# The decay matrix of the gated delta rule: eight broadcast products, or a scaled triangle and two wide ones

## The chip, the cores and the metric

The kernel runs on one core of one Trainium2 chip. The metric is the device time of one execution in microseconds. TensorE multiplies matrices, VectorE, ScalarE and GpSimd work element by element, and the sync engine's queue issues the weight transfers.

## The reference

A stack of blocks over 256 tokens with model width 1024: two mixer layers with a gated feed-forward block before and behind each, then an even and an odd mixer with their own feed-forward blocks. The weights, some 330 MB of f32, are read once. The change is in the mixer layer, in its gated delta rule branch. Cut to what matters:

```python
GDN_HEADS, GDN_DK, GDN_DV, GDN_CHUNK = 4, 128, 128, 64

def gated_delta_rule_chunked(q, k, v, beta, g):      # 256 tokens, 4 heads, chunks of 64
    gcum = jnp.cumsum(g, axis=-1)
    decay = jnp.exp(jnp.where(tril, gcum[..., :, None] - gcum[..., None, :], NEG_INF))
    a = jnp.where(strict, jnp.einsum('bhnid,bhnjd->bhnij', k_beta, k) * decay, 0.0)
    ...
    qk = jnp.einsum('bhnid,bhnjd->bhnij', q, k) * decay
```

The kernel works on blocks of 128 tokens rather than 64. There are eight blocks: 2 token tiles times 4 heads. For each it needs a 128x128 matrix whose entry (i, j) is the cumulated g up to token j, the same in every row i. With a 0/1 triangle T, that is the sum over tokens k of g[k] T[k, j].

## The kernel before

The whole kernel is one program of hand-ordered instruction streams, one for each engine, that wait for one another through semaphores. There is no planner.

*Weights.* They come as units of 128x1024 f32 (512 KB). The sync queue loads unit u into one of 3 raw buffers (L482) as soon as VectorE has split unit u-3. ScalarE copies it to `w_hi` (`split`, L539), rounding it, and VectorE subtracts to get the rest, `w_lo` (L1193). There are 6 slots of split weights, and the splits run 5 units ahead of TensorE (`AHEAD`). TensorE multiplies each unit in three passes, high by high, high by low and low by high (L2137 is the helper through which nearly all products are recorded). A unit of the gdn projection takes it 24 products of 256 columns.

*The mixer layer, as far as the change goes.* TensorE works through the units of `small`, `moba_q`, `gdn` (12 units), then a turn of latents (`cT`), four units `moba(1)`, the sums of squares `stat` (16 products with one column), the step `R`, the products of k with k (`G`), four units `moba(2)`, then the triangular solve. Meanwhile:

- VectorE computes g (`sc[:, 240:248]`, 128 tokens by 8 blocks; L1535 to L1543, event `g`), right before the pair loop over the gdn units. In each of the six rounds of that loop it splits two weight units (L1193), runs the convolution on two channels (L1559, six instructions of 256 columns) and the gating of the round before (L1570). After it come the last gating (event `silu`) and the rest of the latents (`c_lo`, L1596).
- ScalarE copies weights (L539) and the projection's results (L732, L735), and after `silu` squares q and k in one instruction (L769, event `gsq`). TensorE's `stat` waits for it.
- GpSimd computes reciprocal roots (L1108: `crs`, then `grs` after event `gvar`, which follows `stat`), and later in the solve five mask products of 128x512 (L1123). Between the mixers and the even mixer it prepares a filter with four products of 128x1024 (L1155).
- The step `R`: for each of the eight blocks TensorE loads the column of g, broadcast to 128 columns, as weights, and multiplies the 128x128 triangle `tri`. The result goes to banks 6 and 7 of PSUM. It waits for `c_lo`, which frees these banks. VectorE then forms the exponent in `E` (L1618, event `Et`).

Every f32 product (operands not rounded) shows as two records in the trace.

`arena[:, 3072:4096]` holds `zs` later in the layer (the z gate, written after the step QKT).

Of the kernel before, what the change touches and what calls it, by code (L numbers as in the profile page):

```python
# [21 lines left out]
ALU = mybir.AluOpType  # L22
AX = mybir.AxisListType

PART = 128
# [30 lines left out]
LEVELS = 7  # L56
# [162 lines left out]
class Events:  # L219
# [8 lines left out]
    def sig(self, l, step):  # L228
# [11 lines left out]
                "mlavark", "qrope", "mlak", "mlavarq"])  # L240
ACT_STEPS = (["sm", "spe", "csq", "cn", "egc", "kds", "c_hi", "gsq", "E", "AT", "QKT", ("U", 1), "mobasq"] + [s for s in LV_STEPS if s[0] == "U" and s[1] > 1]
             + ["u1", "wT", "O0", "osq", "mobaT", "oz_hi", "ksq", "qcopy", "qsq", "vcopy", "qT0", "qT1", "kT0", "kT1"])
POOL_STEPS = (["crs", "grs"] + [("ATM", m) for m in range(1, 4)] + ["mobars"] + [("ATM", m) for m in range(4, LEVELS - 1)]
              + ["ors", "mlarsk", "mlarsq"])


# [6 lines left out]
def build(nc, stream, params, consts, late_in, x_in, out):  # L253
    with ExitStack() as ctx:
        def sb(name, shape, dt=F32):
            return ctx.enter_context(nc.sbuf_tensor(name, shape, dt))

        def sem(name):
            return ctx.enter_context(nc.semaphore(name))
# [11 lines left out]
        ones = sb("ones", [PART, PART])  # L271
        nhalf = sb("nhalf", [PART, 64])
        sc = sb("sc", [PART, 512])
# [30 lines left out]
        act_ev = [Events(sem("act_step"), ACT_STEPS)]  # L304
        pool_ev = [Events(sem("pool_step"), POOL_STEPS)]
        PE, DV, AC, PO = pe_ev[0], dve_ev[0], act_ev[0], pool_ev[0]
# [41 lines left out]
        def const(name, i=0, n=None):  # L348
            lo, hi = CONST[name]
            return con[:, lo + i:(hi if n is None else lo + i + n)]  # L350
# [3 lines left out]
        def bank(b, lo=0, hi=512):  # L354
            return ps[:, b, lo:hi]

        def flat(ap):
            return ap.rearrange("p a b -> p (a b)")

        def over(ap, n):  # L360

            return ap.unsqueeze(2).broadcast_to([PART, ap.shape[1], n])

        def each(ap, n):

            return ap.unsqueeze(1).broadcast_to([PART, n, ap.shape[1]])


        def reg(lo, *dims):
            n = int(np.prod(dims))  # L370
            v = arena[:, lo:lo + n]
            return v if len(dims) == 1 else v.rearrange("p (a b) -> p a b", b=dims[-1])

        gup = gates[:, 8:24, :].rearrange("p a b -> p (a b)")
        mqkv = reg(0, 6, 512)
        zs = reg(3072, 4, TOK)
        y = reg(4096, 12, TOK)
        yth = reg(7168, 12, TOK)
        X, XTh = reg(7168, 8, 64), reg(7680, 8, 64)
# [18 lines left out]
        ATM = [tmpf[:, 0:1024].rearrange("p (a b) -> p a b", b=128), tmpf[:, 1024:2048].rearrange("p (a b) -> p a b", b=128)]  # L398
# [701 lines left out]
        @block.gpsimd  # L1100
        def _(pool):
            chain = [0]
            nc.gpsimd.memset(nhalf[:], -0.5).then_inc(pool_chain, 1)
            pool.wait_ge(pool_chain, 1)

            def rsqrt(o, i):
                n = i.shape[1]
                return nc.gpsimd.tensor_tensor(o, i, nhalf[:, 0:n], ALU.pow)  # L1108

            def norm(t):  # L1110
                pool.wait_ge(var_ready, t + 1)
                rsqrt(sc[:, 4:6], sc[:, 2:4]).then_inc(rs_ready, 1)

            def mixer(l):
                pool.wait_ge(*DV.at(l, "cvar"))
                rsqrt(sc[:, 228:232], sc[:, 224:228]).then_inc(*PO.sig(l, "crs"))
                pool.wait_ge(*DV.at(l, "gvar"))
                rsqrt(sc[:, 112:128], sc[:, 128:144]).then_inc(*PO.sig(l, "grs"))
                pool.wait_ge(*AC.at(l, "AT"))
                for m in range(1, LEVELS - 1):  # L1120
                    if m >= 3:
                        pool.wait_ge(*PE.at(l, ("U", m - 2)))
                    nc.gpsimd.tensor_tensor(ATMh[m % 2], ATh, each(const("mt", (m - 1) * 64, 64), 8), ALU.mult  # L1123
                                            ).then_inc(*PO.sig(l, ("ATM", m)))
                    if m == 3:
                        pool.wait_ge(*DV.at(l, "mobavar"))
                        rsqrt(sc[:, 192:224], sc[:, 160:192]).then_inc(*PO.sig(l, "mobars"))
                pool.wait_ge(*DV.at(l, "ovar"))
                rsqrt(sc[:, 152:160], sc[:, 144:152]).then_inc(*PO.sig(l, "ors"))
                pool.wait_ge(*DV.at(l, "mlavark"))  # L1130
                rsqrt(sc[:, 208:224], sc[:, 176:192]).then_inc(*PO.sig(l, "mlarsk"))
                pool.wait_ge(*DV.at(l, "mlavarq"))
                rsqrt(sc[:, 192:208], sc[:, 160:176]).then_inc(*PO.sig(l, "mlarsq"))

            t = 0
            for l in range(DEPTH):
                norm(t); t += 1
                norm(t); t += 1
                mixer(l)
                norm(t); t += 1  # L1140

            n_taps = 4 * TAP_STEP * TAP_GROUPS
            pool.wait_ge(mix_ready, 4 * DEPTH)
            nc.gpsimd.memset(wcomp, 0.0).then_inc(taps_set, 1)
            pool.wait_ge(taps_loaded, 16 * TAP_STEP)
            pool.wait_ge(taps_set, 1)
            for j in range(TAP_STEP):
                r, m = slice(TAP_ROWS * j, TAP_ROWS * (j + 1)), len(range(j, CFK, TAP_STEP))
                for i in range(4):
                    o = wcomp[r, TAP_STEP * TAP_GROUPS * i:TAP_STEP * TAP_GROUPS * (i + 1)].rearrange("p (q g) -> p q g", g=TAP_GROUPS)  # L1150
                    nc.gpsimd.tensor_copy(o[:, :, 0:m], wrep[r, :, CFK * i + j:CFK * (i + 1):TAP_STEP]).then_inc(taps_set, 1)
            pool.wait_ge(taps_set, 1 + 4 * TAP_STEP)
            for c in range(4):
                part = slice(n_taps // 4 * c, n_taps // 4 * (c + 1))
                nc.gpsimd.tensor_tensor(wtap[:, part, :], each(const("rows"), n_taps // 4), over(wcomp[:, part], TAP_ROWS), ALU.mult  # L1155
                                        ).then_inc(taps_set, 1)
            norm(t); t += 1

            pool.wait_ge(*DV2.at(0, "lnvar"))
            rsqrt(sc[:, 276:278], sc[:, 278:280]).then_inc(*PO2.sig(0, "lnrs"))  # L1160
            norm(t); t += 1
            norm(t); t += 1
            for i in "kq":
                pool.wait_ge(*DV2.at(0, f"dvar{i}"))
                rsqrt(drs[i], dss[i]).then_inc(*PO2.sig(0, f"drs{i}"))
            norm(t)
# [968 lines left out]
        def _(pe):  # L2135
            def mm(o, a, b, start=True, stop=True, **k):
                return nc.tensor.matmul(o, a, b, start=start, stop=stop, **k)  # L2137
# [241 lines left out]
            def mixer(l, t):  # L2379
                ev = lambda s, st: pe.wait_ge(*s.at(l, st))  # L2380
# [34 lines left out]
                for qk in range(2):  # L2415
                    for tt in range(2):
                        for h in range(4):
                            c = qk * 8 + tt * 4 + h
                            i = mm(bank(0, c, c + 1), tmp[:, qk * 4 + h, 128 * tt:128 * tt + 128], ones[:, 0:1])
                i.then_inc(*PE.sig(l, "stat"))  # L2420
                ev(DV, "c_lo")
                for b in range(8):
                    i = mm(bank(6 + b // 4, 128 * (b % 4), 128 * (b % 4) + 128), sc[:, 240 + b:241 + b].broadcast_to([PART, 128]), const("tri"))
                i.then_inc(*PE.sig(l, "R"))
                kT = lambda tt, h: y[:, 4 + h, 128 * tt:128 * tt + 128]
                qT = lambda tt, h: y[:, h, 128 * tt:128 * tt + 128]
# [49 lines left out]
                m = LEVELS - 1  # L2476
                ev(DV, ("X", m - 1))
                for b in range(8):
                    i = mm(ps[64:128, 1, 64 * b:64 * b + 64], ATx[0:64, b, :], X[0:64, b, :])
# [4 lines left out]
                for b in range(8):  # L2484
                    i = mm(ps[0:64, 4, 64 * b:64 * b + 64], U[64:128, b, :], XT[64:128, b, 64:128])
# [50 lines left out]
                for n in range(2):  # L2536
                    for j in range(TT):
# [4 lines left out]
                        i = mm(o, a_lo[:, 10, tk], w_hi[:, s, w], start=False, stop=True)  # L2542
# [6 lines left out]
                for j in range(TT):  # L2549
                    tk = slice(128 * j, 128 * j + 128)  # L2550
                    for k in range(2):
# [3 lines left out]
                        i = mm(o, a_lo[:, 8 + k, tk], w_hi[:, s, w], start=False, stop=(k == 1))  # L2555
# [218 lines left out]
            for l in range(DEPTH):  # L2774
                ffn(POS["ffa", l], F, t); F += FT; t += 1
                mixer(l, t); t += 1
                ffn(POS["ffb", l], F, t); F += FT; t += 1
# [121 lines left out]
```

## Time and profile before

| | |
|---|---|
| median of 3 runs | 1989.17 us (1986.13 to 1991.87) |
| span of the profiled execution | 1983.2 us |
| TensorE matmul busy | 1952.0 us (98%) |
| TensorE weight loads busy | 1818.2 us (92%) |
| VectorE busy | 1491.1 us (75%) |
| ScalarE busy | 1083.7 us (55%) |
| GpSimd busy | 96.1 us (5%) |
| mean granted TensorE clock | 0.996 |

The busy times are sums over the whole span. Engines work at the same time, and their waits are told apart by the chain of waits and the timeline. The granted clock is given as a share of full speed: 1.00 is 2.4 GHz, 0.50 is 1.2 GHz.

### The profile page before, as it was taken

To read this page: it belongs to the slowest core of one execution; us is meant where nothing else is said; L and a number is where in the kernel's file an instruction comes from. 1 tells how busy PE (TensorE), PEld (TensorE's weight loads), DVE (VectorE), ACT (ScalarE), POOL (GpSimd) and SP (SyncE) were. 2 spreads that over 40 slices of the span, in tenths; PEclk is the share of its full clock that TensorE was granted. 3 is DMA by queue.
4 is the path that set the end of the run, shared out by engine and by line. 5 is a ranking of instruction groups with operands and counts; after the bars stand their busy time and mean duration, and the time that the engine had idled before them with its cause. 6 is when DMAs were issued, how large, how long until landed. Compare 5 with 4: busy or idle time off the path is not lost.

```text
span 1983.2 us, 38420 instructions
## 1 busy us (share of the span) xinstructions
PE 1952.0 (98%) x14681; PEld 1818.2 (92%) x14681; DVE 1491.1 (75%) x2306; ACT 1083.7 (55%) x1714; POOL 96.1 (5%) x61
## 2 busy tenths in 40 slices
PE   9999999999999999999999999999999999999999
PEld 8999899999999999998899999999899999889998
DVE  6777877667777777778767778777578888877887
ACT  5455664664545554556546644555345555765554
POOL 0000002010000000000120103000000000100000
PEclk9999999999999999999999999999999999999999
DMA  6555443344555555555424454555745555534554
GB/s 228 184 185 194 161 155 108 108 156 146 158 188 189 193 167 184 188 170 181 140 85 141 142 170 151 192 187 178 211 163 179 190 183 167 170 127 139 191 190 138
DMA packets 95799, 331.04 MB, mean 167 GB/s; under 512 B 10960, under 2 KB 16720, under 8 KB 95568
## 3 DMA queue, kind: packets, MB, share of 16 engines
q1 hardware_dynamic: 93712, 325.91, 50.3%
q10 hardware_dynamic: 1984, 3.68, 0.5%
q8 instruction: 74, 1.21, 0.3%
q14 instruction: 29, 0.24, 0.0%
HBM read 327.91 MB, written 1.64 MB: 166 GB/s over the span
## 4 chain that ended last, share of the span: by engine, by line
PE 83%; DVE 8%; ACT 3%; DMA 2%; issue 1%; POOL 1%; SPq 0%; DVEq 0%; ACTq 0%
PE ps L2137 82%; DVE w_lo L1193 3%; DMA raw<-stream 2%; ACT w_hi L539 1%; POOL sc L1108 1%; ACT a_both L565 1%; DVE arena L1559 1%; PE ps L2348 1%; ACT tmp L568 0%; PE ps L2562 0%; DVE x L1204 0%; POOL tmp L1123 0%; DVE tmp L1289 0%; DMA x<-x_in 0%; PE ps L2715 0%
## 5 line engine op out<-in xcount | busy, mean ns | idle before, releaser
L2137 PE MATMUL ps<-a_both,w_hi 128*128 128x256 f32 (+1 forms) x7104 | 1402.9, 312 | 9.6 <-ACT a_both L565 3.0
L2137 PEld LDWEIGHTS ps<-a_both,w_hi 128*128 128x128 f32 x7104 | 1158.8, 191 | 85.4 <-ACT a_both L565 4.0
L2137 PE MATMUL ps<-a_both,w_lo 128*128 128x256 f32 x4464 | 978.5, 283 | 0.0
L1193 DVE TENSOR_TENSOR w_lo<-raw,w_hi 128x1024 fp32r<-128x1024 f32 x614 | 750.1, 1228 | 244.3 <-ACT w_hi L539 243.9
L2137 PEld LDWEIGHTS ps<-a_both,w_lo 128*128 128x128 f32 x4464 | 739.8, 191 | 8.9
L539 ACT ACTIVATE w_hi<-raw 128x1024 fp32r<-128x1024 f32 x614 | 634.4, 1050 | 160.9 <-DMA raw<-stream 102.5
L1108 POOL TENSOR_TENSOR sc<-sc,nhalf 128x2 f32<-128x2 f32 (+5 forms) x25 | 66.0, 2641 | 1656.8 <-DVE sc L1221 1223.4
L2137 PE MATMUL ps<-w_hi,a_both 128*128 128x512 f32 (+2 forms) x464 | 140.0, 379 | 4.1 <-DVE w_lo L1193 2.8
L608 ACT ACTIVATE a_both<-arena 128x256 fp32r<-128x256 f32 x132 | 55.2, 418 | 138.3 <-DVE arena L1310 108.1
L597 ACT ACTIVATE arena<-arena 128x256 f32<-128x256 f32 x88 | 36.8, 418 | 169.4 <-DVE arena L1302 143.9
L1267 DVE TENSOR_TENSOR arena<-ps,arena 128x512 f32<-128x512 f32 x114 | 78.8, 691 | 54.8 <-ACT arena L602 54.5
L602 ACT ACTIVATE arena<-ps 128x512 f32<-128x512 f32 x114 | 67.9, 595 | 83.6 <-PE ps L2137 83.6
L2137 PEld LDWEIGHTS ps<-w_hi,a_both 128*128 128x128 f32 x464 | 86.3, 189 | 20.0 <-DVE w_lo L1193 3.7
L2137 PE MATMUL ps<-w_lo,a_both 128*128 128x512 f32 (+2 forms) x232 | 86.9, 375 | 0.0
L1302 DVE TENSOR_TENSOR arena<-arena 128x512 f32<-128x512 f32 x114 | 78.0, 684 | 0.0
L891 ACT ACTIVATE arena<-arena,par 128x256 f32<-128x256 f32 x44 | 26.5, 602 | 93.0 <-DVE arena L1302 78.2
L1315 DVE TENSOR_TENSOR a_both<-arena,a_both 128x256 fp32r<-128x256 f32 x132 | 56.7, 430 | 6.3 <-ACT a_both L608 6.3
L2137 PE MATMUL ps<-arena 128*128 128x128 f32 (+4 forms) x400 | 52.4, 327 | 3.0 <-DVE arena L1702 1.7
L2137 PEld LDWEIGHTS ps<-w_lo,a_both 128*128 128x128 f32 x232 | 44.0, 189 | 6.6
L2137 PEld LDWEIGHTS ps<-arena 128*64 128x64 f32 (+2 forms) x400 | 38.6, 172 | 12.4 <-DVE arena L1702 2.0
L1802 DVE SCALAR_TENSOR_TENSOR arena<-arena,par 128x255 f32<-128x255 f32 x44 | 21.3, 484 | 38.0 <-ACT arena L891 38.0
L655 ACT ACTIVATE gates<-ps 128x256 f32<-128x256 f32 x48 | 18.5, 386 | 41.1 <-PE ps L2137 40.7
(319 smaller groups left out, 1252.4 us busy)
## 6 DMA issues: line engine op xcount, KB each, us to landing
raw<-stream SPq DMA_DIRECT2D x613, 512.0 KB, 3.4
arena<-upad SPq DMA_DIRECT2D x8, 284.0 KB, 6.0
gates<-late ACTq DMA_DIRECT2D x1, 1088.0 KB, 7.2
out<-x SPq DMA_DIRECT2D x8, 128.0 KB, 2.0
upad<-arena ACTq DMA_DIRECT2D x2, 288.0 KB, 5.6
con<-consts SPq DMA_DIRECT2D x1, 560.0 KB, 5.1
raw<-stream ACTq DMA_DIRECT2D x1, 512.0 KB, 3.8
x<-x_in SPq DMA_DIRECT2D x2, 256.0 KB, 5.0
```

Of the source, the lines that this page charges most:

```text
L539: nc.scalar.activation(w_hi[:, u % SLOTS, :], raw[:, u % RAW, :], ACT.Copy).then_inc(hi_ready, 1)
L597: nc.scalar.activation(th2[:, p, :], gus[:, p, 0:TOK], ACT.Tanh, scale=0.5).then_inc(gate_act, 1)
L602: nc.scalar.activation(glo, ps[:, 4 + 2 * p:6 + 2 * p, TOK:512], ACT.Copy).then_inc(lo_copied, 1)
L608: nc.scalar.activation(a_hi[:, 8 + p, :], gu2[:, p, :], ACT.Copy).then_inc(gu_hi_ready, 1)
L891: nc.scalar.activation(gh2[:, p, :], gus[:, p, 0:TOK], ACT.Identity, scale=w, bias=b).then_inc(conv_in, 1)
L1108: return nc.gpsimd.tensor_tensor(o, i, nhalf[:, 0:n], ALU.pow)
L1193: V.tensor_tensor(w_lo[:, u % SLOTS, :], raw[:, u % RAW, :], w_hi[:, u % SLOTS, :], ALU.subtract).then_inc(split_ready, 1)
L1267: V.tensor_tensor(gus[:, p, :].rearrange("p (a b) -> p a b", b=TOK), ps[:, 4 + 2 * p:6 + 2 * p, 0:TOK], glo, ALU.add).then_inc(gu_added, 1)
L1302: V.tensor_tensor(v, v, each(rrow, 2), ALU.mult).then_inc(gs_ready, 1)
L1315: V.tensor_tensor(a_lo[:, 8 + p, :], gu2[:, p, :], a_hi[:, 8 + p, :], ALU.subtract).then_inc(gu_split, 1)
L1802: V.scalar_tensor_tensor(gh2[:, p, 1:], gus[:, p, 0:TOK - 1], w[1], gh2[:, p, 1:], ALU.mult, ALU.add).then_inc(loop_chain2, 1)
L2137: return nc.tensor.matmul(o, a, b, start=start, stop=stop, **k)
```

## The change

GpSimd gets a new step `gtri` after `crs`: it waits for `g` and multiplies the triangle, repeated eight times, with the eight columns of g, each spread over 128 columns. The result, 128x1024 f32, lies in `arena[:, 3072:4096]`. TensorE's step `R` waits for it and multiplies it in two products of 512 columns with a 128x128 matrix of ones as weights, one for each bank. The eight products with a broadcast column are gone. `grs` now stands behind `gtri` in GpSimd's stream. Everything else stays.

```diff
-POOL_STEPS = (["crs", "grs"] + [("ATM", m) for m in range(1, 4)] + ["mobars"] + [("ATM", m) for m in range(4, LEVELS - 1)]
+POOL_STEPS = (["crs", "gtri", "grs"] + [("ATM", m) for m in range(1, 4)] + ["mobars"] + [("ATM", m) for m in range(4, LEVELS - 1)]
@@
         zs = reg(3072, 4, TOK)
+        gtri = reg(3072, 8, 128)
@@ GpSimd, mixer(l)
                 rsqrt(sc[:, 228:232], sc[:, 224:228]).then_inc(*PO.sig(l, "crs"))
+                pool.wait_ge(*DV.at(l, "g"))
+                nc.gpsimd.tensor_tensor(gtri, each(const("tri"), 8), over(sc[:, 240:248], 128), ALU.mult).then_inc(*PO.sig(l, "gtri"))
                 pool.wait_ge(*DV.at(l, "gvar"))
@@ TensorE, mixer(l, t)
                 ev(DV, "c_lo")
-                for b in range(8):
-                    i = mm(bank(6 + b // 4, 128 * (b % 4), 128 * (b % 4) + 128), sc[:, 240 + b:241 + b].broadcast_to([PART, 128]), const("tri"))
+                ev(PO, "gtri")
+                for tt in range(2):
+                    i = mm(bank(6 + tt), ones[:], flat(gtri[:, 4 * tt:4 * tt + 4, :]))
                 i.then_inc(*PE.sig(l, "R"))
```

`each(ap, n)` repeats a block n times and `over(ap, n)` spreads each column over n columns, both by a step of zero.

## Rows read from the trace of the kernel before

**Rows 1.** The page, part 1: busy us (share of the span) xinstructions.

```profile
PE 1952.0 (98%) x14681; PEld 1818.2 (92%) x14681; DVE 1491.1 (75%) x2306; ACT 1083.7 (55%) x1714; POOL 96.1 (5%) x61
```

**Rows 2.** The chain of waits, layer 1: start us, us, what.

```profile
238.15 2.27 DVE w_lo L1193 x2
240.42 2.38 DVE arena L1559 x6
...
266.44 4.33 DMA raw<-stream
...
271.18 0.57 issue
271.75 1.91 ACT tmp L769
```

**Rows 3.** Stretches: length, busy (instructions) by engine, PEclk, DMA share, GB/s.

```profile
212.00:238.00 26.00, 24.12 (x149) 21.10 (x147) 19.03 (x48) 15.29 (x27) 1.71 (x2) 1.00 0.55 182
238.00:273.70 35.70, 35.38 (x251) 33.11 (x251) 35.67 (x68) 27.33 (x46) 0.00 (x0) 1.00 0.59 192
```

**Rows 4.** Timeline of weight loads, stat, R, G, both layers: start, us, what [idle before].

```profile
273.70 4.03 PEld L2137 LDWEIGHTS ps<-ones,tmp 128*128 128x128 f32 x32 [0.54 <-ACT tmp L769]
277.61 3.53 PEld L2137 LDWEIGHTS ps<-con,sc 128*128 128x128 f32 x16
281.02 3.15 PEld L2137 LDWEIGHTS ps<-arena 128*128 128x128 f32 x16
...
955.46 3.65 PEld L2137 LDWEIGHTS ps<-ones,tmp 128*128 128x128 f32 x32 [0.37 <-ACT tmp L769]
959.03 3.06 PEld L2137 LDWEIGHTS ps<-con,sc 128*128 128x128 f32 x16
961.97 2.35 PEld L2137 LDWEIGHTS ps<-arena 128*128 128x128 f32 x16
```

**Rows 5.** Stretches with the clock: layer 1 (TensorE alone), layer 2 (all engines).

```profile
276.00:276.90 0.90, 0.90 (x10) 0.99 0.99 396
...
277.00:283.50 6.50, 6.50 (x31) 0.50 0.22 74
...
960.00:962.80 2.80, 2.80 (x15) 2.80 (x14) 0.40 (x2) 0.43 (x1) 2.39 (x1) 0.50 0.27 111
```

**Rows 6.** Stretches, weight loads alone: R's in layer 2, G's in layer 1.

```profile
958.95:959.55 0.60, 0.52 (x5) 1.00 1.10 178
...
282.00:283.40 1.40, 1.40 (x8) 0.50 0.00 0
```

**Rows 7.** Timeline of TensorE: the layer norm's mean, and what follows.

```profile
1438.24 1.89 PE L2137 MATMUL ps<-arena,ones 128*128 128x256 f32 x8
1439.78 0.47 PE L2137 MATMUL ps<-a_both,w_hi 128*128 128x256 f32 x1
```

**Rows 8.** Timeline of GpSimd.

```profile
278.11 2.90 POOL L1108 TENSOR_TENSOR sc<-sc,nhalf 128x16 f32<-128x16 f32 x1 [42.51 <-DVE sc L1610]
...
307.92 1.32 POOL L1123 TENSOR_TENSOR tmp<-gates,con 128x512 f32<-128x512 f32 x1 [7.23 <-PE ps L2137]
...
323.47 2.99 POOL L1123 TENSOR_TENSOR tmp<-gates,con 128x512 f32<-128x512 f32 x1
...
1199.14 9.68 POOL L1155 TENSOR_TENSOR gates<-con,gates 128x1024 f32<-128x1024 f32 x4
```

**Rows 9.** Timeline of VectorE beside GpSimd's products.

```profile
324.10 1.22 DVE L1193 TENSOR_TENSOR w_lo<-raw,w_hi 128x1024 fp32r<-128x1024 f32 x1
...
1199.45 1.88 DVE L1315 TENSOR_TENSOR a_both<-arena,a_both 128x256 fp32r<-128x256 f32 x1 [0.48 <-ACT a_both L608]
...
1201.86 5.19 DVE L1193 TENSOR_TENSOR w_lo<-raw,w_hi 128x1024 fp32r<-128x1024 f32 x2
1206.97 2.13 DVE L1307 SCALAR_TENSOR_TENSOR arena<-arena 128x256 f32<-128x256 f32 x1
...
1210.05 0.43 DVE L1315 TENSOR_TENSOR a_both<-arena,a_both 128x256 fp32r<-128x256 f32 x1 [0.48 <-ACT a_both L608]
```

## The prediction

> **What bounds the kernel now.** I read the page first: TensorE is busy for 98% of the 1983.2 us span, VectorE for 75%, GpSimd for 5% [rows 1]. A microsecond added to TensorE's work or to its waits is therefore a microsecond of the kernel. But that is an average over stages, and the change sits at one place of each of the two mixer layers. So next I read the chain of waits around the first layer's place [rows 2]. From 238 to 266 us it does not run over TensorE: it runs through VectorE (weight splits L1193, convolution L1559, gating L1570, back to back), then one weight transfer of 4.33 us that waited for a split to free its buffer, then ScalarE's copy and its square L769 at 271.75, and only then to TensorE's sums at 273.70. The table of stretches says the same: VectorE is busy for 35.67 of the 35.70 us from 238.0 to 273.7 [rows 3]. TensorE is fed there from weights split ahead, but it gets to the end early and waits for the square: "0.54 <-ACT tmp L769" in the first layer, 0.37 in the second [rows 4]. So in these 36 us VectorE has no slack towards TensorE, and what is added to its path comes out at that wait.
>
> Then the replaced step itself [rows 4]. The 16 weight loads of the eight products (two records each) start from 277.61 to the next group's 281.02, 3.41 us, in layer 1, and from 959.03 to 961.97, 2.94 us, in layer 2. The granted clock explains the difference: it is 0.50, the 1.2 GHz level, from 277.0 to 283.5 in layer 1 and from 960.0 to 962.8 in layer 2 [rows 5], each time after some 3 us of one-column sums.
>
> **The change, part by part.**
>
> *Eight products of 128 columns become two of 512.* At half clock a record of 128 columns takes 3.41 / 16 = 0.213 us; at the full one 5 of them lie in 0.60 us, 0.12 us each [rows 6]. The trace has no f32 product of 512 columns. The nearest are the layer norm's f32 products of 256 columns with the same ones as weights, at full clock: 8 records from 1438.24 to 1439.78, 0.193 us each [rows 7]. A record of one column takes (959.03 - 955.46) / 32 = 0.112 us [rows 4], so that is a floor, and 256 columns lie well above it. If cost goes with columns, 512 take 0.386 us at full and 0.77 us at half clock, and four records 1.54 and 3.09 us. If 128 columns at half clock are already bound by columns, four records take 4 x 4 x 0.213 = 3.41 us. What streams through the array is 16 x 128 columns before and 4 x 512 after, the same 2048. So the gain is between 0 and 3.41 - 3.09 = 0.3 us at half clock, and between 0 and 16 x 0.12 - 1.54 = 0.4 us at full clock. The G step next to it, which has no broadcast operand, begins 8 loads in 1.40 us at half clock, under 0.2 us each [rows 6]; so the broadcast costs next to nothing either. I take a gain of 0.1 us a layer, nearer the column bound, because the stretch runs mostly at half clock.
>
> *TensorE's new wait for GpSimd.* The product can start when g is ready, at about 238.1 (the splits behind it on VectorE start at 238.15 [rows 2]), and TensorE wants it at 277.6. GpSimd had been idle for 42.51 us when it took up its next work at 278.11 [rows 8]. The product, and the reciprocal root queued behind it, are covered by more than 30 us: nothing is paid. If the product came late, TensorE would wait with all its later steps behind it, but that takes a product of 39 us. No DMA is issued or moved.
>
> *GpSimd's product, as VectorE feels it.* This is the term that I charge. At 1199.14 GpSimd runs four products of exactly this size and kind of operands (a repeated constant times a spread column, 128x1024) in 9.68 us [rows 8]. VectorE instructions with two operands in SBUF meet them [rows 9]: L1315 takes 1.88 us, against 0.43 once GpSimd is done; two splits take 5.19 us, against 1.22 for one elsewhere; L1307, as large as L1315, takes 2.13. The excess is 1.45 + 2.75 + 1.70 = 5.9 us for four products, 1.5 each, and 1.7 where VectorE queues right behind. L1315 came 0.31 us after the first product's start, so the product kept it out until 1.45 + 0.31 = 1.76 us after its own start. At 238.1 VectorE runs two such splits, then L1559, which also has two SBUF operands, with no gap [rows 2]. Whether GpSimd gets in after the first split or later, VectorE loses about one product: I take 1.7 us, with 1.45 and 2.6 as bounds (twice the 1.32 us of the mask product of 512 columns [rows 8]).
>
> The Trainium skill's page "SBUF — State Buffer", section "Who interferes with whom", has the rule that speaks against this edit: a VectorE instruction with two SBUF inputs and a GpSimd instruction that reads SBUF exclude one another, each for a whole instruction. By that rule the trace agrees (1.88 against 0.43 us). By the skill's "GPSIMD Engine Reference", section "3.1 Elementwise — side-by-side cycle accounting", such a product costs about 2.6 cycles an element, an estimate of 2.2 us for 1024; with it the sum would be 1993.4.
>
> *What the 1.7 us is worth.* With 0.03 us idle in the stretch every later VectorE step moves by 1.7, the split that frees the buffer of the last transfer too, and with it transfer, copy and square. The cover ahead of TensorE is gone already (0.54 and 0.37 us waited). By VectorE alone the square might have started up to 0.57 us sooner (the "issue" row [rows 2]); if that is slack, 1.45 - 0.57 = 0.9 us is left, the low bound. I charge the full 1.7. Behind the sums everything follows TensorE, so nothing gives it back.
>
> *The sum.* 2 layers x (1.7 - 0.1) = +3.2 us: span 1983.2 to 1986.4. The median of the runs, 1989.17, lies 6.0 above the span of the profiled execution; I carry the 6.0 over: **1992.4 us**. With the bounds: 2 x (0.9 - 0.4) = +1.0 to 2 x 2.6 = +5.2, so 1990.2 to 1994.4.
>
> **Rivals.**
>
> 1. *The product costs VectorE nothing (0.16).* GpSimd is kept out while VectorE runs back to back, and works only in gaps. For it: at 323.47 a mask product takes 2.99 instead of 1.32 us [rows 8], beside a split that takes its usual 1.22 [rows 9]. Against it: the stretch has no gap, so GpSimd would have to wait 35 us, and at 1201.86 it did get in between two adjoining splits. Time: 1989.2 less at most 0.8, so 1988.8.
>
> 2. *The clock falls sooner (0.15), the slow side.* The wait before the sums grows from 0.54 to 2.2 us. The sums take 3.91 us in layer 1, whose last 0.7 us are at half clock (0.99 granted until 276.9 [rows 5]), and 3.57 in layer 2: a record costs double, 0.22, at half clock. If the clock is at half from the sums' start, they take 32 x 0.22 = 7.0 us: +3.1 and +3.4, so 1992.4 + 6.5 = 1998.9. It decides only if 2 us of waiting lower the clock. Against it: from 212 to 238 TensorE is idle for 1.88 us and the clock stays at 1.00 [rows 3].
>
> 3. *The clock returns sooner (0.12).* If it is back with the first of the long products, R and G run at 0.12 a record: in layer 1 they save 6.5 - 32 x 0.12 = 2.7 us, in layer 2, with 2.8 us at half clock, 1.4. Time: 1992.4 - 4.1 = 1988.3. Against it: the same columns stream as before, and the clock came back only during G.
>
> 4. *The change does not do what it says (0.03):* something else in the mixer reacts, either way.
>
> **How the numbers follow.** The forecast has 0.54, at 1992.4. A measurement of this kernel can tell about 0.3%, 6.0 us, from no change. Of the forecast's 0.54 I give 0.06 to slower, for a price at the upper bound and the scatter of the runs (1986.1 to 1991.9). Slower: 0.06 + 0.12 of rival 2 + 0.01 = 0.19. Faster: 0.04, rival 3 without the contention. Same: 0.77. The range goes from 1987.0, which takes in rivals 1 and 3 with the runs' scatter, to 1999.0, which takes in rival 2.
>
> **What would show it.** Right: a split or L1559 at 238 to 242 us stretched by 1.5 to 2 us in all, the waits for L769 grown from 0.54 and 0.37 to about 2.2 and 2.0 us, R as four records of about 0.8 us at half clock. Wrong: no stretched VectorE row there; or a stretched one and the wait unchanged, since then there was slack that I do not see; R clearly under 3 us at half clock; the half-clock stretch moved or changed in length.

## The result, and the profile after

The changed kernel takes 1994.63 us (median of 7 runs, 1993.73 to 1996.79), the kernel before on the same chip 1987.90 us (7 runs, 1985.08 to 1991.87). The ratio is 1.003, 95% interval 1.0021 to 1.0039: slower by 6.0 us, and by 4.2 to 7.8 with the interval. The forecast was 1992.4 in a range of 1987.0 to 1999.0, with 0.77 on a change too small to be told from none (0.3%, 6.0 us). The measured time lies inside the range, and the change is at the edge of that 0.3%, with an interval that leaves 1 out.

The page of the changed kernel, parts 1 (busy times) and 5 (costliest groups), shows nothing that would catch the eye (the span is 1993.6 us); the splits L1196 (L1193 before) are 3.7 us busier in all, 3.4 of which are the two places below:

```profile
PE 1954.7 (98%) x14657; PEld 1816.2 (91%) x14657; DVE 1494.6 (75%) x2306; ACT 1083.7 (54%) x1714; POOL 101.5 (5%) x63
...
L1196 DVE TENSOR_TENSOR w_lo<-raw,w_hi 128x1024 fp32r<-128x1024 f32 x614 | 753.8, 1234 | 244.9 <-ACT w_hi L540 244.2
```

So one has to go to the place. The timeline of GpSimd and of VectorE there, in layer 1 and layer 2 (start, length, what), and last the second split of layer 1 by itself:

```profile
239.15 2.81 POOL L1119 TENSOR_TENSOR arena<-con,sc 128x1024 f32<-128x1024 f32 x1 [2.63 <-DVE sc L1546]
...
925.04 2.81 POOL L1119 TENSOR_TENSOR arena<-con,sc 128x1024 f32<-128x1024 f32 x1 [2.63 <-DVE sc L1546]
...
238.99 4.06 DVE L1196 TENSOR_TENSOR w_lo<-raw,w_hi 128x1024 fp32r<-128x1024 f32 x2
242.97 2.45 DVE L1562 SCALAR_TENSOR_TENSOR arena<-gates,par,arena 128x256 f32<-128x256 f32 x6
...
924.87 4.06 DVE L1196 TENSOR_TENSOR w_lo<-raw,w_hi 128x1024 fp32r<-128x1024 f32 x2
...
240.12 2.92 DVE L1196 TENSOR_TENSOR w_lo<-raw,w_hi 128x1024 fp32r<-128x1024 f32 x1
```

Two splits take 4.06 us instead of 2.35: 1.71 us more in each layer, in layer 1 all of it in the second one (2.92 us instead of 1.22), and the instructions behind them on VectorE keep their length. The timeline of weight loads, the rows that answer to [rows 4]:

```profile
276.81 6.78 PEld L2140 LDWEIGHTS ps<-ones,tmp 128*128 128x128 f32 x32 [2.73 <-ACT tmp L770]
283.48 0.55 PEld L2140 LDWEIGHTS ps<-arena,ones 128*128 128x128 f32 x2
284.54 0.34 PEld L2140 LDWEIGHTS ps<-arena,ones 128*128 128x128 f32 x1 [0.52 <-issue]
285.39 0.34 PEld L2140 LDWEIGHTS ps<-arena,ones 128*128 128x128 f32 x1 [0.52 <-issue]
...
288.83 0.19 PEld L2140 LDWEIGHTS ps<-w_hi,a_both 128*128 128x128 f32 x1
...
963.08 6.90 PEld L2140 LDWEIGHTS ps<-ones,tmp 128*128 128x128 f32 x32 [3.11 <-ACT tmp L770]
969.86 0.55 PEld L2140 LDWEIGHTS ps<-arena,ones 128*128 128x128 f32 x2
...
975.07 0.19 PEld L2140 LDWEIGHTS ps<-w_hi,a_both 128*128 128x128 f32 x1
```

And the stretches with the granted clock (the last three columns are clock, DMA share, GB/s; TensorE alone), which answer to [rows 5]:

```profile
274.50:276.50 2.00, 0.00 (x1) 1.00 0.65 213
277.00:287.00 10.00, 10.00 (x36) 0.50 0.35 105
287.50:289.00 1.50, 1.50 (x16) 1.00 0.00 0
...
963.50:973.00 9.50, 9.50 (x35) 0.50 0.36 110
```

From these rows the loss can be counted, from the last weight load ahead of the wait to the first load of the units behind G (before: 284.10 and 964.23 in the same timeline).

| us | layer 1 before | after | layer 2 before | after |
|---|---|---|---|---|
| wait for the square | 0.54 | 2.73 | 0.37 | 3.11 |
| one-column sums | 3.91 | 6.67 | 3.57 | 6.78 |
| R and G | 6.49 | 5.35 | 5.20 | 5.21 |
| sum | 10.94 | 14.75 | 9.14 | 15.10 |

That is +3.8 and +6.0, 9.8 of the 10.4 us between the two profiled spans: 4.9 from the waits, 6.0 from the sums at half clock, 1.1 given back behind them. The medians are only 6.7 apart. The profiled execution of before was quick: each run of the changed kernel lies 1.8 us above its span (1995.36 against 1993.6), so a span of 1983.2 belongs to a run of about 1985.0, while the median is 1987.9. Other executions of the kernel before spend longer at half clock: of its 100 timed executions in the experiments, the 11 with a mean granted clock of 0.994 or less took 1988.6 us on average, the 32 at 0.997 or more 1984.8. Part of the clock loss is there already; in which stretch, the one profile of that kernel does not show.

### The profile page after: what moved, and what is told of

Read it like the earlier page. It is cut to its first block, busy times and chain, and to the rows that moved or that the text cites. A ratio compares the mean times of both kernels' runs of the same rounds, so it can differ in the third digit from the quotient of the medians.

```text
span 1993.6 us, 38376 instructions
## 1 busy us (share of the span) xinstructions
PE 1954.7 (98%) x14657; PEld 1816.2 (91%) x14657; DVE 1494.6 (75%) x2306; ACT 1083.7 (54%) x1714; POOL 101.5 (5%) x63
## 3 DMA queue, kind: packets, MB, share of 16 engines
HBM read 327.91 MB, written 1.64 MB: 165 GB/s over the span
## 4 chain that ended last, share of the span: by engine, by line
PE 81%; DVE 9%; ACT 4%; DMA 3%; issue 1%; POOL 1%; SPq 0%; DVEq 0%; ACTq 0%
PE ps L2140 80%; DVE w_lo L1196 4%; DMA raw<-stream 2%; ACT w_hi L540 2%; DVE arena L1562 1%; POOL sc L1109 1%; ACT a_both L566 1%; PE ps L2351 1%; ACT tmp L569 0%; PE ps L2566 0%; DVE x L1207 0%; POOL tmp L1126 0%; DVE tmp L1292 0%; DMA x<-x_in 0%; DVE arena L1264 0%
## 5 line engine op out<-in xcount | busy, mean ns | idle before, releaser
L1196 DVE TENSOR_TENSOR w_lo<-raw,w_hi 128x1024 fp32r<-128x1024 f32 x614 | 753.8, 1234 | 244.9 <-ACT w_hi L540 244.2
```

The source lines that it names most:

```text
L1196: V.tensor_tensor(w_lo[:, u % SLOTS, :], raw[:, u % RAW, :], w_hi[:, u % SLOTS, :], ALU.subtract).then_inc(split_ready, 1)
```

## The experiments

All ratios are against the kernel before on the same chip, with the 95% interval in brackets. Each profile is that of one execution, which can be one of the quick or one of the long ones of its kernel.

### The product without the wide form: pool_alone

```diff
-                for tt in range(2):
-                    i = mm(bank(6 + tt), ones[:], flat(gtri[:, 4 * tt:4 * tt + 4, :]))
+                for b in range(8):
+                    i = mm(bank(6 + b // 4, ...), sc[:, 240 + b:241 + b].broadcast_to([PART, 128]), const("tri"))
```

> GpSimd's product and TensorE's wait for it as in the changed kernel, but the step R with its eight broadcast products as before; the product's result is computed and not used. Theory (the product holds VectorE up by 1.7 us a layer, that lengthens the wait before the sums, and the wait brings the clock to its half level before the sums): about 1994.6, as the changed kernel, with the two splits at 4.06 us, the wait for L770 near 2.7 and 3.1 us and the sums near 6.7 us in the profile. Rival (the two wide products or their form cost the time): about 1988, as before.

1993.02 us, ratio 1.0025 (1.0014 to 1.0036). The profiled execution was the longest, 1996.70. The two splits take 4.05 us. The wait is 3.61 and 3.36 us, and the sums take 6.1 us in both layers:

```profile
276.96 6.24 PEld L2140 LDWEIGHTS ps<-ones,tmp 128*128 128x128 f32 x32 [3.61 <-ACT tmp L770]
283.07 3.53 PEld L2140 LDWEIGHTS ps<-con,sc 128*128 128x128 f32 x16
...
963.03 6.22 PEld L2140 LDWEIGHTS ps<-ones,tmp 128*128 128x128 f32 x32 [3.36 <-ACT tmp L770]
```

The product alone brings the loss, within the uncertainty all of it. The narrow R takes 3.4 us here, as long as the wide one.

### The product later: late_product

```diff
-                pool.wait_ge(*DV.at(l, "g"))
+                pool.wait_ge(*DV.at(l, "c_lo"))
```

> The changed kernel, with one event changed: GpSimd's product waits for c_lo instead of g, so it runs after VectorE's last step on the path to the square. Theory: VectorE is not held up between g and the square, the wait before the sums goes back to about 0.5 us, TensorE still finds the product ready (it needs 2 us from about 272.4, and R starts at 277.6): about 1987.9, as before, perhaps 0.2 less. Rival (the wide form of R costs the time): stays near 1994.6.

1986.31 us, ratio 1.0002 (0.9993 to 1.0011): no difference that the interval can tell. The loss is not in the wide form of R, but in where the product stands. The timeline of GpSimd and VectorE shows something more:

```profile
273.06 4.75 POOL L1119 TENSOR_TENSOR arena<-con,sc 128x1024 f32<-128x1024 f32 x1 [36.78 <-DVE a_both L1599]
...
272.90 0.89 DVE L1606 TENSOR_TENSOR arena<-con,par 128x128 f32<-128x128 f32 x4
273.71 2.35 DVE L1196 TENSOR_TENSOR w_lo<-raw,w_hi 128x1024 fp32r<-128x1024 f32 x2
```

Here the splits keep their 2.35 us and GpSimd is the one kept out: its product ends at 277.81, 1.75 us after VectorE's last split. R starts at 278.67, so it still finds its operand, with under 0.9 us to spare.

### Two products: double_product

```diff
+                nc.gpsimd.tensor_tensor(kgd, each(const("tri"), 8), over(sc[:, 240:248], 128), ALU.mult)
                 nc.gpsimd.tensor_tensor(gtri, each(const("tri"), 8), over(sc[:, 240:248], 128), ALU.mult).then_inc(*PO.sig(l, "gtri"))
```

> The changed kernel with a second GpSimd product of the same size right ahead of the one used, its result unused. Theory: VectorE is held up twice, 3.4 us a layer instead of 1.7; the wait before the sums grows by another 1.7 us; the sums are at half clock from their start already and can't lose more: 1994.6 + 2 x 1.7 = 1998.0. Rival (GpSimd is shut out or the path has slack after the first product): 1994.6. Rival (the clock's share grows with the wait as well): over 2001.

1999.46 us, ratio 1.0066 (1.0053 to 1.0079), 12.4 us above before, where the changed kernel was 6.7 above its own. The second product holds up the convolution instead of a split (4.10 us instead of 2.46), by 1.64 us, and the waits grow by as much:

```profile
239.10 4.05 DVE L1197 TENSOR_TENSOR w_lo<-raw,w_hi 128x1024 fp32r<-128x1024 f32 x2
243.07 4.10 DVE L1563 SCALAR_TENSOR_TENSOR arena<-gates,par,arena 128x256 f32<-128x256 f32 x6
...
278.48 6.90 PEld L2141 LDWEIGHTS ps<-ones,tmp 128*128 128x128 f32 x32 [4.30 <-ACT tmp L770]
...
966.38 6.54 PEld L2141 LDWEIGHTS ps<-ones,tmp 128*128 128x128 f32 x32 [4.67 <-ACT tmp L770]
```

4.30 and 4.67 against 2.73 and 3.11, +1.6 each. So there is no slack behind the first product. The distance to before rose by 5.7 us in the medians (7.2 by the ratios) instead of the expected 3.4. In the profile the sums did not get longer, but R and G took 6.30 and 5.61 us instead of 5.35 and 5.21, since the half clock lasted into G. The profiled spans differ by 3.3. The other 2.4 us between spans and medians I can't place.

### Half the product: half_product

```diff
-nc.gpsimd.tensor_tensor(gtri, each(const("tri"), 8), over(sc[:, 240:248], 128), ALU.mult) ...
+nc.gpsimd.tensor_tensor(gtri[:, 0:4, :], each(const("tri"), 4), over(sc[:, 240:244], 128), ALU.mult) ...
```

with R as before, as in pool_alone.

> As pool_alone (R with its eight broadcast products), but GpSimd multiplies only four of the eight blocks, 128x512; the result is not used. Theory (VectorE is locked out for the length of the product): the two splits take 2.35 + 0.9 = about 3.2 us, the wait before the sums is 1.4 to 2 us, and the time rises by 2 x 0.9 = 1.8 to 1988.8, and by up to 3 us more if this wait brings the clock down before the sums, 1991.8. Rival (GpSimd's use costs a fixed amount): 1993, as pool_alone.

1989.12 us, ratio 1.0016 (1.0007 to 1.0025). The splits take 3.20 us, 0.85 more, half of 1.71:

```profile
238.97 1.96 POOL L1119 TENSOR_TENSOR arena<-con,sc 128x512 f32<-128x512 f32 x1 [2.63 <-DVE sc L1546]
238.81 3.20 DVE L1196 TENSOR_TENSOR w_lo<-raw,w_hi 128x1024 fp32r<-128x1024 f32 x2
...
275.14 5.31 PEld L2140 LDWEIGHTS ps<-ones,tmp 128*128 128x128 f32 x32 [1.27 <-ACT tmp L770]
...
958.85 6.26 PEld L2140 LDWEIGHTS ps<-ones,tmp 128*128 128x128 f32 x32 [2.50 <-ACT tmp L770]
```

The hold-up goes with the size of the product. With the wait of layer 1 (1.27) the sums are 1.3 us longer than before, with the one of layer 2 (2.50) 2.6 us: here the longer wait goes with more of the sums at half clock.

### GpSimd busy without reading: memset_alone

```diff
-nc.gpsimd.tensor_tensor(gtri, each(const("tri"), 8), over(sc[:, 240:248], 128), ALU.mult) ...
+nc.gpsimd.memset(arena[:, 3072:4096], 0.0) ...
```

with R as before.

> As pool_alone (R with its eight broadcast products), but GpSimd fills the 128x1024 block with zeros, which reads nothing from SBUF, instead of multiplying; the block is not used. Theory (what excludes VectorE is GpSimd's reading, as its second operand is read on the same way): the two splits stay at 2.35 us, the time at 1987.0. Rival (any GpSimd instruction at this place holds VectorE up, or its writes do): the splits stretch by the length of the fill, about 1 us, and the time rises by 2 us or more.

1987.48 us, ratio 1.0 (0.999 to 1.0011). The fill lies right beside a split and neither notices:

```profile
237.98 0.95 POOL L1119 MEMSET arena<- 128x1024 f32 x1 [2.60 <-DVE sc L1546]
237.84 2.35 DVE L1196 TENSOR_TENSOR w_lo<-raw,w_hi 128x1024 fp32r<-128x1024 f32 x2
...
954.96 4.99 PEld L2140 LDWEIGHTS ps<-ones,tmp 128*128 128x128 f32 x32 [1.45 <-ACT tmp L770]
```

So not every instruction of GpSimd holds up VectorE: of the two kinds tried, the one that reads SBUF does. This is how the Trainium skill states it ("SBUF — State Buffer", section "Who interferes with whom"), and this run agrees: 2.35 us beside a fill, 4.06 beside a product. The last row is a warning: the wait in layer 2 is 1.45 us without any hold-up. The chain there goes over a transfer that took 5.23 us from the split to its landing. The same transfer of layer 2 took 4.14 us in the profile of before, and 5.08 in late_product, which has no hold-up either (wait 1.29 us).

### The wait filled: fill_wait

```diff
+                pe.wait_ge(cb_ready, 6 * l + 6)
+                for _ in range(16):
+                    mm(bank(0, 0, TOK), a_hi[:, 0, 0:128], a_hi[:, 0, :])
                 ev(AC, "gsq")
-                pe.wait_ge(cb_ready, 6 * l + 6)
```

> The changed kernel with 16 products of 256 columns (rounded operands, 0.12 us each, 1.9 us in all) on TensorE in the wait before the sums; their results are overwritten by the sums and not used. Theory: the wait stays as long but is filled, so the clock is full at the start of the sums, which take 3.6 to 3.9 us instead of 6.7: 1994.6 less up to 6 us for both layers, so 1989 to 1992. Rival (the idle wait has nothing to do with the clock, the one-column sums alone bring it down): the sums stay near 6.7 us and the time at 1994.6.

1988.59 us, ratio 1.0012 (1.0003 to 1.0021). VectorE is held up as in the changed kernel (4.05 us), but the sums run at full clock:

```profile
274.63 2.09 PEld L2140 LDWEIGHTS ps<-a_both 128*128 128x128 f32 x16
277.48 3.65 PEld L2140 LDWEIGHTS ps<-ones,tmp 128*128 128x128 f32 x32 [0.75 <-ACT tmp L770]
...
959.04 3.65 PEld L2140 LDWEIGHTS ps<-ones,tmp 128*128 128x128 f32 x32 [0.39 <-ACT tmp L770]
962.61 0.30 PEld L2140 LDWEIGHTS ps<-arena,ones 128*128 128x128 f32 x2
963.15 0.19 PEld L2140 LDWEIGHTS ps<-arena,ones 128*128 128x128 f32 x1 [0.24 <-issue]
963.58 0.19 PEld L2140 LDWEIGHTS ps<-arena,ones 128*128 128x128 f32 x1 [0.24 <-issue]
```

Useless work in the wait wins back 1.0030 - 1.0012 = 0.18%, 3.6 us of the 6.0 (the two intervals together leave 1.0 to 6.2). So the clock is a large part of the change's price, and it is the idle wait that brings it down ahead of the sums. What is left, 2.4 us, is near what the profile has: the wait grew by 4.5 us in the two layers, and sums, R and G together are 1.7 us shorter than in the profile of before. The last rows give the wide product at full clock: its loads are 0.43 us apart, at half clock 0.85.

### The triangle scaled on ScalarE: act_product

```diff
+                    if p == 2:
+                        act.wait_ge(*DV.at(l, "g"))
+                        for b in range(8):
+                            i = nc.scalar.activation(gtri[:, b, :], const("tri"), ACT.Copy, scale=sc[:, 240 + b:241 + b])
+                        i.then_inc(*AC.sig(l, "gtri"))
```

with GpSimd's product gone and R wide, waiting for ScalarE's `gtri`.

> The changed kernel with the scaled triangle made on ScalarE instead of GpSimd, in eight instructions of 128x128, behind the gating of the third pair; R with two wide products waits for it. Theory (only the exclusion between GpSimd and VectorE costs): ScalarE waits for weights for 7.8 us in this stretch, so its 2.4 us disappear there: the splits stay at 2.35 us for two, the wait at 0.5 us, the time 1987.0. Rival (any work added to the engines of this path delays the square): up to 2 x 2.4 more before the clock, 1992.

1988.18 us, ratio 1.0014 (1.0005 to 1.0023): a miss, slower by 2.8 us. The splits stay at 2.35 us as expected, and layer 1 waits 0.58 us only. But layer 2 waits 2.70 us, and its chain of waits runs over the new instructions (L750) and a slow transfer:

```profile
931.40 2.33 ACT arena L750 x8
933.73 0.96 ACT w_hi L540
...
934.72 2.36 DVE w_lo L1199 x2
...
947.60 6.26 DMA raw<-stream
```

The copy of a weight unit stands right behind the eight instructions, and VectorE waits for it, but not for long: from the first split of the loop to the end of the last it needs 28.48 us (from 919.02) against 28.26 before (920.01 to 948.27). So ScalarE's work costs 0.2 us there, and the transfer, 6.26 us against 4.14, the other 2.1 of the 2.33 us by which the wait grew. Why this transfer was so long, the trace does not show. The miss by 1.2 us against the expected 1987.0 is therefore not shown to come from the work on ScalarE.

### R ahead of the sums: r_first_broadcast

```diff
-                (sums)      ev(DV, "c_lo")      (R, eight products)
+                ev(DV, "c_lo")      (R, eight products)      (sums)
```

This and the next two start from the kernel before.

> The kernel before, without any GpSimd product, with the step R moved ahead of the one-column sums. R needs only g and the banks freed by c_lo (about 272.4 us), not the square. Theory (the wait before the sums idles TensorE and R is paid at half clock behind the sums): R now lies in the 0.5 us wait and runs at full clock, 16 records at 0.12 = 1.9 us instead of 3.4 and 2.9; the sums start about 1.4 us later. Gain a layer about 0.5 (wait) + 1.2 (clock): 1987.0 - 3.4 = 1983.6. Rival (the clock falls as early after the last weights whatever runs in between, or VectorE and ScalarE behind the later sums get late): 1987 or more.

1983.20 us, ratio 0.9987 (0.9978 to 0.9996). R takes 1.90 us in both layers instead of 3.41 and 2.94, and the wait is gone (the profiled execution was the quickest of this kernel):

```profile
273.21 1.98 PEld L2137 LDWEIGHTS ps<-con,sc 128*128 128x128 f32 x16
275.11 3.65 PEld L2137 LDWEIGHTS ps<-ones,tmp 128*128 128x128 f32 x32
278.68 1.87 PEld L2137 LDWEIGHTS ps<-arena 128*128 128x128 f32 x16
```

### R and G ahead of the sums, or among them: rg_first, interleave

In rg_first both steps stand ahead of the sums; in interleave R does, and one product of G follows every second sum.

> The kernel before, with both R (eight broadcast products) and G ahead of the one-column sums. G needs k after its gating, which is there once the last gating (silu) is done. Theory: the wait for the square is gone entirely, R and G run at full clock, 32 records at 0.12 = 3.8 us instead of 6.5 and 5.2; the sums take 3.6 us, and if the clock falls behind them up to 3.3 us of the next units run at half, which costs up to 1.6 us a layer. Sum: layer 1 10.94 to 7.5 to 9.1, layer 2 9.14 to 7.5 to 9.1, so 1986.2 less 1.8 to 5.1: about 1982.7. Rival (the later sums delay the root, the exponent and the solve): 1986 or more.

1983.43 us, ratio 0.9975 (0.9965 to 0.9985), 5.0 us faster than before.

> The kernel before, with R (eight broadcast products) ahead of the sums, and one product of G behind every second sum. Theory: R fills the wait, and the products of G among the sums keep the clock up, so nothing of this stretch and nothing behind it runs at half clock: 64 records at 0.112 to 0.12 us = 7.5 us in both layers instead of 10.94 and 9.14: 1986.2 - 5.1 = 1981.1. Rival (the sums bring the clock down whatever lies among them, since two thirds of the records still have one column): as r_first_broadcast, about 1983.5.

1984.66 us, ratio 0.9988 (0.9979 to 0.9996): faster, but by 2.4 us instead of 5.1. The products of G among the sums did not keep the clock up; it fell at their end all the same (stretches of 2 us, TensorE alone; the units start at 280.44):

```profile
278.00:280.00 2.00, 2.00 (x20) 1.00 0.38 154
280.00:282.00 2.00, 2.00 (x9) 0.56 0.00 0
```

### The change in the better order: gr_first_pool, gr_first_act

G, then the wide R, then the sums, with the product on GpSimd as in the changed kernel, or on ScalarE as in act_product.

> The changed kernel (early GpSimd product, two wide products) with G first, then the wide R, then the one-column sums. Theory: VectorE is still held up by 1.7 us a layer, so silu and c_lo come that much later and TensorE waits for silu for some 0.5 to 1.5 us at about 274; but G and R (3.6 us at full clock) then cover the wait for the square, and no clock falls ahead of them. So of the change's 6 to 7 us about 1 to 3 stay: 1983.4 (rg_first) + 2 = 1985.5. Rival (the wait for the square only moves, as c_lo comes late): 1990 or more.

1983.45 us, ratio 0.9983 (0.9974 to 0.9992).

> As gr_first_pool, with the scaled triangle made on ScalarE (as in act_product). Theory: no lockout of VectorE; ScalarE's 2.3 us come partly through as later transfers, but G and the wide R cover them. The wide R takes 1.7 us at full clock, 0.2 less than eight narrow products: 1983.4 - 0.4 = 1983.0, at most 1 more. Rival (ScalarE's work delays the gating itself and so the start of G): 1985.

1984.60 us, ratio 0.9986 (0.9977 to 0.9995), 1.6 us above the expected 1983.0 and no faster than with the product on GpSimd. In gr_first_pool TensorE waits 0.67 us ahead of G in layer 1, and the square is there once G and R are done:

```profile
273.77 1.86 PEld L2140 LDWEIGHTS ps<-arena 128*128 128x128 f32 x16 [0.67 <-issue]
...
276.95 0.19 PEld L2140 LDWEIGHTS ps<-ones,tmp 128*128 128x128 f32 x1 [0.24 <-issue]
```

With work on TensorE to cover the wait, the same GpSimd product costs no more than the intervals can tell: 0.9983 against rg_first's 0.9975, whose intervals overlap. All versions with R ahead of the sums are faster than both kernels compared here.

## Why the prediction came out as it did

- *GpSimd's product holds up VectorE: 1.7 us a layer.* Right to the hundredth: 4.06 instead of 2.35 us for two splits. It was read from a place 960 us later in the trace, where products of the same size meet splits. pool_alone, half_product, double_product and memset_alone show the cause: the hold-up is there without the wide R, goes with the size of the product, and is absent when GpSimd only writes.
- *It goes on to TensorE in full.* Right, and too low. The waits grew by 2.19 and 2.74 us instead of 1.7. The prediction moved VectorE's path and the last transfer along with their old lengths. Two transfers in the chain of the changed kernel (the first two rows, layer 1 and layer 2) were longer, and in layer 1 a later split waited, through ScalarE's copy, for the first of them:

```profile
262.67 4.92 DMA raw<-stream
...
954.95 5.21 DMA raw<-stream
...
268.71 1.23 DVE L1196 TENSOR_TENSOR w_lo<-raw,w_hi 128x1024 fp32r<-128x1024 f32 x1 [0.82 <-ACT w_hi L540]
```

  The same two transfers took 3.19 us (issued at 260.05) and 4.14 us (948.38) in the profile of before. The one of layer 2 is scatter as far as the profiles tell: it takes 4.1 to 5.5 us in the six kernels in which the product holds VectorE up, and 4.1 to 5.2 in the six with neither a hold-up nor ScalarE's product. The one of layer 1 is not plain scatter: it takes 4.57 us or more in all four profiles with one whole product at 239 us (5.81 in pool_alone) and 3.1 to 3.3 in all others. What it runs into there is open.
- *The wide R gains 0.1 us a layer.* The bound by columns was the right one: the loads are 0.85 us apart at half clock, 4 x 0.853 = 3.41 us, as long as the 16 narrow records. late_product (1.0002, the interval is 1.8 us to each side) shows no gain or price of this part of the change. The 0.3 us at half clock are not there; at full clock R goes from 1.90 to 4 x 0.43 = 1.7 us, 0.2 of the 0.4 at the upper bound.
- *The clock.* This is the step that failed: the sum has no term for it, it stood as rival 2 with 0.15, and it is what happened. The sums run at half clock almost from their start in both layers and take 6.67 and 6.78 us, where rival 2 had 7.0. By the prediction's own signs of being wrong, the half-clock stretch changed in length: some 10 us in each layer instead of 6.8 and 3.4. I weighed the rival down with 1.88 us of idle time at 212 to 238 us that left the clock alone, though the text itself said that the clock falls after some 3 us of the sums alone. Those 1.88 us are a sum over 26 us, and the trace of before has nearer rows, which the prediction does not use. At the kernel's start TensorE waits 2.52 us, until 24.4 us, and near the end 3.01 us (weight loads); both times it goes on at half clock. The second one, with stretches of TensorE alone:

```profile
1748.56 1.78 PEld L2715 LDWEIGHTS ps<-con,arena 128*128 128x128 f32 x9 [3.01 <-DVE arena L2044]
...
1746.00:1748.00 2.00, 0.00 (x0) 1.00 0.35 122
...
1748.60:1751.00 2.40, 2.40 (x12) 0.50 0.00 0
```

  The waits that I expected, 2.2 and 2.0 us, lie between these and the 1.82 us ahead of 222.74 that left the clock at 1.00. Such rows ask for more than 0.15 on a rival whose price is 6.5 us. fill_wait settles the cause: with the wait filled, the sums take 3.6 us.
- *The sum.* Expected +3.2, measured +6.7 by the medians (+6.0 by the ratio). Term by term in the profiles: wait +4.9 instead of +3.4, sums +6.0 instead of 0, R and G -1.1 instead of -0.2. Between the profiled spans rival 2 has 3.2 + 6.5 = 9.7 us, close to the measured 10.4. Its 1998.9 is 4.3 too high through the offset of 6.0 us between span and median: 1.8 belong to every run, the other 4.2 mean that the profiled execution was a quick one.
- *The nearness is in part luck.* 1992.4 is only 2.2 below the measured time although the profiled spans differ by 10.4 us instead of 3.2: the same offset, 4.2 too high, hides much of the missing 7.2. The three runs it was taken from have a median of 1989.17, seven have 1987.9. The range held because it was drawn to take rival 2 in.
- *Rival 1* (GpSimd kept out) did not occur at 239 us, but it did at 273 in late_product. Rival 3 did not occur: the clock came back at 287, during G.

## What to carry to other kernels

Before work goes to an idle engine, look at who shares a way to memory with it at that moment: GpSimd was 95% idle, and 2.8 us of work there in each of two layers cost 6 us of the kernel, since it fell beside the one engine that the next wait hung on. The same product 34 us later cost nothing that could be measured. And look at what stands behind a wait on TensorE: about 3 us of idle time ahead of one-column products cost about as much again through the clock (4.9 us in the profiles, 6.0 less 1.1) as by themselves (4.9). The cure was order: useful work of 128 and more columns (R and G) ahead of the sums, which also beat the kernel before by 0.25%. When a sum has no term for the clock, look for every wait of that length in the trace at hand, and read the granted clock behind it.

## What the runs showed of the hardware

- An f32 product shows as two records. One record took, by columns: 128 columns 0.213 us at half clock, 512 columns 0.853 at half and 0.43 at full; one column takes 0.112 at full and about 0.21 at half (6.67 / 32). So a record of 128 columns (0.12 at full clock) takes hardly longer than one of one column, and from there on the time grows with the columns: merging f32 products of 128 columns gains next to nothing.
- A GpSimd product of 128x1024 that reads SBUF kept a VectorE instruction with two SBUF operands out for 1.71 us, one of 128x512 for 0.85, a fill of 128x1024 not at all.
- Who waits is not plain. Between two adjoining splits GpSimd got in at 239 us, after the first; at 273 us it waited for four small instructions and both splits, 3 us, in both layers. The Trainium skill ("SBUF — State Buffer", section "Who interferes with whom") says that the one that issues first has the way for its whole instruction; what happens when VectorE's instructions follow without a gap, these runs leave open.
- TensorE was busy throughout the sums, by its records, and still the clock went to its 1.2 GHz level: 3.2 us after their start in layer 1 of before, and after 2.5 to 3.6 us of idle time (the changed kernel, pool_alone, half_product, act_product) within 1.0 us of it. After 4.30 us in layer 1 of double_product it was down before they began.
